# A hybrid decoder step with product-key experts on one core: three more places for tile 0's U rows, 87 dots in the second pass, and the samples' x grouped ahead

## The reference

```
x += W_out [ gMLP-chunk(h) || dilated-window-attention(h) ],  h = RMSNorm(x) W_in
x += PEER(RMSNorm(x));   y = RMSNorm(x)
```

```python
q = (xb @ w_q).reshape(TOK_BLK, PEER_HEADS, 2, DK_HALF)          # 8 heads, 2 halves of 128
s = jnp.einsum('thcd,hcnd->thcn', q, sub_keys)                   # 128 scores per half
s1, i1 = lax.top_k(s[:, :, 0], TOPK); s2, i2 = lax.top_k(s[:, :, 1], TOPK)
cand = (s1[..., :, None] + s2[..., None, :])                     # 16 x 16 sums
top_s, pos = lax.top_k(cand, TOPK)                               # 16 experts per head
eid = jnp.take_along_axis(cid, pos, axis=-1)
g = jax.nn.softmax(top_s, axis=-1)
hid = gelu(jnp.einsum('thkd,td->thk', u_tab[eid], xb))
y = jnp.einsum('thk,thkd->td', g * hid, v_tab[eid])
```

## Time and profile before

| | before |
|---|---|
| median of 3 runs | 1666.52 us (1664.41 to 1666.96) |
| the profiled execution | 1670.37 us |
| its span | 1668.6 us |
| mean granted clock of TensorE | 0.971 |
| busy: PE, DVE, ACT, POOL | 1390.3, 1077.4, 635.6, 654.5 us |
| moved by DMA | 664.81 MB, 398 GB/s over the span |

### The profile page before, as it was taken

How to read it: one execution, slowest core, us unless ns; L and a number is a source line. 1 busy time by engine, 2 the same in 40 slices (tenths; PEclk the granted TensorE clock), 3 DMA queues, 4 the chain that set the end, 5 groups by cost and what they waited for, 6 DMA issues and landing times.

```text
span 1668.6 us, 17631 instructions
## 1 busy us (share of the span) xinstructions
PE 1390.3 (83%) x5164; PEld 616.0 (37%) x5164; DVE 1077.4 (65%) x2770; ACT 635.6 (38%) x1911; POOL 654.5 (39%) x703
## 2 busy tenths in 40 slices
PE   8999995888999988888887877777878777777786
PEld 5585663444334444343322322222223222222211
DVE  1469968877100158677766666666668888888654
ACT  1421113455111045444444544444445444444443
POOL 3035434333467643333343333333333333333331
PEclk9999997899999999999999999999999999999999
DMA  9799989999999999999999999999999999999995
GB/s 340 299 370 383 336 324 395 360 422 382 402 400 400 410 419 419 421 421 421 421 422 421 421 422 421 422 421 421 421 421 420 421 423 417 418 421 414 417 381 246
DMA packets 111567, 664.81 MB, mean 398 GB/s; under 512 B 13008, under 2 KB 14272, under 8 KB 51824
## 3 DMA queue, kind: packets, MB, share of 16 engines
q0 software_dynamic: 97824, 571.76, 84.0%
q1 hardware_dynamic: 13648, 91.93, 13.9%
HBM read 658.04 MB, written 5.60 MB: 398 GB/s over the span
## 4 chain that ended last, share of the span: by engine, by line
DMA 51%; PE 30%; issue 7%; DVE 7%; ACT 5%; POOL 1%; ACTq 0%; DVEq 0%; SPq 0%; POOLq 0%
DMA area_r<-in_uv_tab,eid 41%; PE bank L950 7%; PE bank L667 7%; DMA area_c<-in_uv_tab,eid 5%; PE bank L894 4%; PE bank L939 4%; PE bank L832 3%; ACT area_v L1052 2%; DMA area_r<-in_uv_tab,eidT 1%; DMA area_w<-in_w_out 1%; DMA area_w<-in_uv_tab,eid 1%; PE bank L598 1%; DVE area_r L1759 1%; PE bank L808 1%; DVE area_x L1767 1%
## 5 line engine op out<-in xcount | busy, mean ns | idle before, releaser
L950 PE MATMUL bank<-area_r,area_v 128*128 128x512 f32 (+1 forms) x1032 | 506.1, 620 | 138.5 <-ACT area_v L1052 132.7
L1938 POOL DMA_INDIRECT area_r<-in_uv_tab,eid x383 | 364.4, 951 | 650.6 <-PE bank L950 370.0
L1759 DVE CUSTOM_DVE_ANT_0 area_r<-area_r,bank 128x1024 f32<-128x1024 f32 x275 | 334.5, 1217 | 202.6 <-DMA area_r<-in_uv_tab,eid 202.0
L950 PEld LDWEIGHTS bank<-area_r,area_v 128*128 128x128 f32 (+1 forms) x1032 | 177.9, 187 | 459.2 <-issue 452.8
L1306 ACT ACTIVATE area_v<-hid 128x1 f32<-128x1 f32 x416 | 83.8, 201 | 523.7 <-DVE hid L1759 523.1
L950 PE MATMUL bank<-area_w,area_v 128*128 128x512 f32 (+1 forms) x384 | 190.2, 624 | 54.8 <-ACT area_v L1052 54.5
L1938 POOL DMA_INDIRECT area_w<-in_uv_tab,eid x116 | 110.3, 951 | 179.4 <-PE bank L950 154.0
L667 PE MATMUL bank<-area_w,area_t 128*128 128x384 f32 (+1 forms) x448 | 157.5, 508 | 3.7 <-DMA area_w<-in_w_in 3.1
L1052 ACT ACTIVATE area_v<-ident,area_v 128x128 f32<-128x128 f32 x364 | 146.1, 401 | 33.8 <-PE bank L950 0.4
L1759 DVE CUSTOM_DVE_ANT_0 area_w<-area_w,bank 128x1024 f32<-128x1024 f32 x96 | 116.8, 1217 | 63.7 <-DMA area_w<-in_uv_tab,eid 63.2
L1938 POOL DMA_INDIRECT area_r<-in_uv_tab,eidT x128 | 121.7, 951 | 76.4 <-issue 31.3
(11 more groups left out here) (208 smaller groups left out, 1429.2 us busy)
## 6 DMA issues: line engine op xcount, KB each, us to landing
area_w<-in_w_in SPq DMA_DIRECT2D x12, 1536.0 KB, 10.2
area_w<-in_k_cache SPq DMA_DIRECT2D x8, 1920.0 KB, 11.9
area_w<-in_v_cache SPq DMA_DIRECT2D x8, 1920.0 KB, 10.7
area_w<-in_w_q SPq DMA_DIRECT2D x14, 1024.0 KB, 8.8
area_w<-in_w_out SPq DMA_DIRECT2D x4, 2048.0 KB, 15.2
area_r<-in_uv_tab,eid POOLq DMA_INDIRECT x383, 18.6
area_x<-in_x_p SPq DMA_DIRECT2D x6, 512.0 KB, 17.8
area_w<-in_w_in SPq DMA_DIRECT2D x2, 1024.0 KB, 8.2
```

The lines of the kernel that those rows point to most:

```text
L950: mm = pe.matmul(acc[0:n, c, :], diag[by_pe(i) % DG][:, 0:n], x_ring[s][:, D + c * 512:D + (c + 1) * 512], start=(i == 0), stop=False, ski ...
L1759: vec.tensor_tensor_reduce(out=u, in0=u, in1=x_cur, scale=1.0, scalar=0.0, op0=ALU.mult, op1=ALU.add, accum_out=hid[t % 2][:, j:j + 1]).th ...
L1938: nc.gpsimd.indirect_dma_start(out=place, out_offset=None, in_=table, in_offset=bass.IndirectOffsetOnAxis(ap=where, axis=0)).then_inc(land ...
```

## The change

It has two halves.

Tile 0's rows: three more places, in the part of `area_w` behind the pieces of W_in. Place 9 is where the scores of tile 0's heads 0 to 3 were and is open from row 52 on, place 10 where those of heads 4 to 7 were (from row 108), place 11 the work area of the routing chain (from row 110). The first row of each waits until the scores there are used: `eid_ready` 4 for place 9, 8 for places 10 and 11. The second pass has 87 dots instead of 80. Head 7's chain begins at group 5 of the attention instead of 7. The second load of the query weights, which comes into the area of places 9 and 10, waits in addition for all 128 dots.

The samples: x of the samples is written into a tile of its own (`x_group`, in the place of tile 1's x) by four copies, one in each of the heads 2 to 5 of tile 3, and `set_x` then makes one copy of it. The gathers of pairs have twelve places instead of ten from row 96 on; the two new ones are where the transposed features were (`area_t`).

```diff
--- before.py
+++ after.py
@@ -49,8 +49,8 @@
 TOPK = 16
 SLOTS = HEADS * TOPK
 UR, VR, XR = 6, 12, 6
-U_EXTRA = ((6, 56), (9, 66), (26, 76))
-XR_ALL, X_MORE, X_WIDER = 10, 6, 96
+U_EXTRA = ((6, 56), (9, 66), (26, 76), (52, SLOTS), (108, SLOTS), (110, SLOTS))
+XR_ALL, X_MORE, X_WIDER = 12, 6, 96
 DG = 4
 RING = 3
 
@@ -61,9 +61,9 @@
 FIRST = [sum(STEPS[:t]) for t in range(NT)]
 NSTEP = sum(STEPS)
 
-DOTS_FIRST, DOTS_PROJ = 12, 80
+DOTS_FIRST, DOTS_PROJ = 12, 87
 ROUTE_PROJ = {1: 2, 6: 3, 12: 4, 18: 5}
-ROUTE_ATT = {1: 6, 7: 7}
+ROUTE_ATT = {1: 6, 5: 7}
 ROUTE_STEP = {8: [9, 10]} | {g: [g + 2] for g in range(9, 24)} | {g: [2 * g - 22, 2 * g - 21] for g in range(24, 31)}
 TOPS_ATT, EID_SAMPLE = 15, 5
 EARLY_GROUPS = 8
@@ -121,7 +121,8 @@
         qT = cut(area_r, 0, PAIRS, TOK)
         kT = cut(area_r, PAIRS * TOK, PAIRS, TOK)
         u_ring = [cut(area_r, 2 * PAIRS * TOK + s * D, D) for s in range(UR)]
-        u_extra = [cut(area_w, (s + 1) % RING * PIECE + KD * HALF, D) for s in range(RING)]
+        u_extra = ([cut(area_w, (s + 1) % RING * PIECE + KD * HALF, D) for s in range(RING)]
+                   + [cut(area_w, RING * PIECE + s * D, D) for s in (1, 2, 3)])
 
 
         def u_places():
@@ -140,7 +141,8 @@
         x_ring = ([cut(area_r, s * 2 * D, 2 * D) for s in range(XR // 2)]
                   + [cut(area_r, 2 * PAIRS * TOK + (V_TURN // 2 + s) % (UR // 2) * 2 * D, 2 * D) for s in range(XR // 2)]
                   + [cut(area_c, 0, 2 * D)]
-                  + [cut(area_w, 2 * PIECE + a, 2 * D) for a in (0, WQ, 2 * WQ + D)])
+                  + [cut(area_w, 2 * PIECE + a, 2 * D) for a in (0, WQ, 2 * WQ + D)]
+                  + [cut(area_t, s * 2 * D, 2 * D) for s in range(2)])
         keys = cut(area_r, 2 * PAIRS * TOK + UR * D, 2 * HEADS * NKEYS)
         h_stage = u_ring
         xn_first = u_ring[UR - 1]
@@ -171,6 +173,7 @@
         u_tok = cut(area_v, NT * DB, NT, DA)
         vn = cut(area_v, NT * (DB + DA), NT, DA)
         xn_tile = [xn_first] + [cut(area_v, (t - 1) * D, D) for t in range(1, NT)]
+        x_group = cut(area_v, 0, D)
         y_junk = cut(area_v, NT * D, D)
 
         logc = cut(area_c, 0, 512)
@@ -269,7 +272,7 @@
         q_done, q_copied = [sem(f"q_done{c}") for c in range(2)], [sem(f"q_copied{c}") for c in range(2)]
         s_done, s_ready = sem("s_done"), sem("s_ready")
         tops_exped, tops_less, head_least = sem("tops_exped"), sem("tops_less"), sem("head_least")
-        u_landed = [sem(f"u_landed{s}") for s in range(UR + RING)]
+        u_landed = [sem(f"u_landed{s}") for s in range(UR + len(U_EXTRA))]
         v_landed = [sem(f"v_landed{s}") for s in range(VR)]
         x_landed = [sem(f"x_landed{s}") for s in range(XR_ALL)]
         x_free, hid_ready, bent_ready, col_ready, diag_ready = (sem("x_free"), sem("hid_ready"), sem("bent_ready"),
@@ -570,6 +573,7 @@
             for t in range(2, NT):
                 load_x(t)
             sp.wait_ge(route_link, HEADS * LINKS)
+            sp.wait_ge(u_free, UR + SLOTS)
             for h in range(3):
                 load_wq(wq_ring[h], h, wq_again[h])
             sp.wait_ge(vn_ready, NT)
@@ -1723,8 +1727,7 @@
                 if t < SAMP:
                     ins = vec.tensor_copy(x_cur, xn_tile[t])
                 else:
-                    for g in range(GROUPS):
-                        ins = vec.tensor_copy(x_cur[g * NSAMP:(g + 1) * NSAMP, :], xn_tile[t][0:NSAMP, :])
+                    ins = vec.tensor_copy(x_cur, x_group)
                 then(ins)
 
             def routings(ks):
@@ -1903,6 +1906,9 @@
                     go_on(links)
                     if g == HEADS:
                         finish_head(HEADS + 1)
+                    if t == SAMP - 1 and 2 <= h < 2 + GROUPS:
+                        a = (h - 2) * NSAMP
+                        then(vec.tensor_copy(x_group[a:a + NSAMP, :], xn_tile[SAMP][0:NSAMP, :]))
                     if h == 1:
                         finish_y(t - 1)
                     if g == 30:
@@ -1952,8 +1958,10 @@
                     pool.wait_ge(u_free, UR)
                 elif s < UR + 2:
                     pool.wait_ge(q_done[1], 2 * (s - UR + 2))
+                elif s == UR + 2:
+                    pool.wait_ge(proj_done, units_through(NC))
                 else:
-                    pool.wait_ge(proj_done, units_through(NC))
+                    pool.wait_ge(eid_ready, HEADS // 2 if s == UR + RING else HEADS)
                 gather(u_row(s), single, eid[:, i:i + 1], u_landed[s])
 
             def gather_v(j):
```

## The result

The changed kernel takes 1681.05 us (median of four runs, 1680.37 to 1683.34). The kernel before took 1666.18 us beside it (four runs, 1664.41 to 1666.96). The ratio over the runs of both is 1.0079, with a 95% interval of 1.0065 to 1.0094. The change makes the kernel slower, by 14.9 us between these two medians and by 13.2 us by the ratio; what follows goes by ratios. The forecast was 1660.2 us, faster, with a range that ended at 1668.0.

The account below looks back on a forecast made before the run. The prediction took nearly everything from 412 us on to go by bytes (DMA). Its terms, +2 + 3.7 - 5 - 6.5 - 0.5 = -6.3 us, took the median from 1666.52 to 1660.2 us, range 1652.5 to 1668.

Parts of the forecast that it names:

- The second pass: Projection, 119 to 255 us: seven more dots fit mostly into DVE's waits; last dot about 2 us later, bounds -2 and +6.
- A new wait: Attention, after head 6's numbers: DVE stops for row 96's landing, 3.7 us at best (taken), 11.6 us at worst.
- Rival 3: Slower, chance 0.12: head 6's first row late, wait 11.6 instead of 3.7 us, PE at lower clock; +4.1, 1670.6 us.
- The wait of row 108: Attention: row 108 waits for head 7's numbers, holding POOL for two groups with nine rows out; no stall.
- The deeper ring: Rest of the attention: ring 7 to 9 deep instead of 6, row waits go; -5 us, bounds 0 and 7.7.
- The tail: Attention's end: 4 us off the last V cache load, 2.5 us off the stretch to the last output product; -6.5 us.
- The samples' rows: Samples' boundary, 1590 to 1595 us: one copy replaces four, the slowest engine sets the landings; -0.5 us, bounds -2.6 and 0.
- the mean of the engines: Samples' boundary: if this counts and not the slowest engine, the hole gives 2.6 us; sign: 3 us or more back.
- The four copies in tile 3: Heads 2 to 5: at most 1.23 us each, hidden by DVE's idle time; each delays one gather's issue, sum unchanged.

## Why the prediction was wrong

**The second pass (+2 us, bounds -2 and +6).** The wait of 8.04 us is gone, as forecast. But the last dot of the pass starts at 268.05 instead of 260.82, 7.2 us later, beyond my upper bound. I let three dots come after the old wait and let that wait shrink. In fact DVE catches up with the rows again at the end: rows 84, 85 and 86 wait 4.19, 0.94 and 0.95 us. "Nothing else waits for DVE there" was wrong too: PE's scores of the attention's second group wait for the first masks that stand behind the last dot, 15.06 us instead of 6.42, and the granted clock in 260 to 280 us was 0.50 against 0.62. The runs put 3.2 to 3.5 us on this (0.9991 and 0.9993 against 0.9972, with 0.1% on each of the three). That it is near what I took is luck; its source was another.

**A new wait (+3.7 us, up to 11.6).** This is the step that failed, by the most: 14.3 to 14.7 us in place of 3.7. Place and cause were right: row 96, right after head 6's numbers, GpSimd idle for 18 us ahead of it, and the wait even shorter than forecast (2.28 us; the gather landed in 299.17 - 295.02 = 4.15 us). The price was wrong, because I priced one landing. What the seven dots use up is the stock of rows: before, six rows (88 to 93) are asked for and not yet used when the numbers come; after, one (row 95). The next rows all leave in one burst and land among each other and the V cache load, and "the later gathers follow 1.25 us apart and are wanted less often" took no account of that: rows 99 and 100 wait 3.42 and 3.15 us, the masks behind them come late, and PE stands for 10.46 us. Taking the stop away with all 87 dots in place is worth 14.3 us (head 6 in the pass) or 14.7 us (fewer dots before head 6). Rival 3 had the direction and PE's stop, with 0.12; it put the price into a late landing of row 96, which did not happen.

**The wait of row 108 ("no stall").** Wrong: GpSimd waits 10.81 us, and DVE then waits 2.91, 3.14 and 2.25 us for rows 108, 112 and 113. Of the nine rows that I had out, seven were out when GpSimd stopped and four when the numbers came, and row 108 then took 11.3 us to its dot. Yet by itself this wait costs nothing that can be measured: with head 6 in the pass it has the same 10.81 us, four rows in stock when the numbers come, and 2.76 us of waiting for row 108, and the kernel takes 0.9993, as without that wait (0.9991). With head 7 two groups later it is 21.89 us, no row is left, and 4.5 us are added; at 80 dots and with head 7 in group 7 it is 2.53 us and the kernel is among the fastest.

**The deeper ring (-5 us).** Right in size, but only without the seven dots. With 80 dots one place takes 0.41% off and three take 0.28 to 0.41% (0.9972, 0.9966 and 0.9959 in three kernels that do not differ beyond their intervals), 5 to 7 us. With 87 dots and head 7 in group 7 three places bring nothing (1.0106 with them, 1.0102 without), and the waits for rows that I took to go rise from 11.9 to 25.9 us (19.8 without the last dots of the pass).

**The tail (-6.5 us, 2 to 10).** Wrong. From the last V cache load to the last product it now takes 427.60 - 405.40 = 22.2 us, before 411.85 - 391.95 = 19.9. PE starts on that load 9.6 us after its issue instead of 10.5, so 0.9 us came of my 4. From there to the last product it takes 12.6 us instead of 9.4: the same last products take 1.98 us where they took 1.09, with 0.54 of the clock granted in 420 to 428 us and 1.00 before in 402 to 412. The run with the samples' half alone has 1.98 us there too and no loss of time, so these 3.2 us may be of this execution only. The dots that left the last groups had cost nothing there that can be measured: with 76 dots, four more in the attention, the ratio is that of 80. In those groups they were covered by PE and the caches, which I had not tested by a row.

**The samples' rows (-0.5 us).** Right as far as it can be told: the hole is filled and the time stays (1.000 within 0.001), which leaves room for -0.5 us and for nothing, and none for the 2.6 us by the mean of the engines. In the profiled execution the rows did move by what was forecast: in the run with the samples' half alone six rows take 1606.07 - 1591.19 = 14.9 us where the earlier trace rows had 15.4.

```profile
1591.19 1.22 DVE L1761 CUSTOM_DVE_ANT_0 area_r<-area_r,bank 128x1024 f32<-128x1024 f32 x1 [1.25 <-DMA area_r<-in_uv_tab,eid]
...
1606.07 1.22 DVE L1761 CUSTOM_DVE_ANT_0 area_r<-area_r,bank 128x1024 f32<-128x1024 f32 x1 [1.23 <-DMA area_r<-in_uv_tab,eid]
```

The four copies in tile 3 take 0.67 to 0.94 us each, not 1.23. In the run with the samples' half alone the gather beside one takes 1.31 us where the next one takes 0.94, and the next starts on time all the same (the copy on VectorE, then the two gathers on GpSimd):

```profile
1416.98 0.68 DVE L1910 COPY area_v<-area_v 32x1024 f32<-32x1024 f32 x1
```

```profile
1416.48 1.31 POOL L1943 DMA_INDIRECT area_c<-in_uv_tab,eid  x1 [1.56 <-PE bank L953]
1418.97 0.94 POOL L1943 DMA_INDIRECT area_r<-in_uv_tab,eid  x1 [1.18 <-PE bank L953]
```

The rule of the Trainium skill (SBUF — State Buffer, the box in "SBUF: two separate sides") that such a copy keeps GpSimd from writing descriptors agrees with this. It is seen beside three of the four copies (1.20, 1.31 and 1.30 us), each time with the gather's end 0.13 us behind the copy's. Beside the fourth the gather takes its 0.94 us and the copy 0.94 instead of 0.68. Other gathers between 1330 and 1510 us take up to 1.17 us without such a copy beside them. It costs 0.3 to 0.4 us of a queue that waits over 1 us for the next place anyway, and so changes no time, as the prediction had it.

In sum, the seven dots cost 1.07% with the change's places and head 7 (1.0079 - 0.9972), and 1.02% in the kernel before. Of the 1.07%, some four fifths are the stop at head 6 with too little stock (0.86 to 0.88%, each within about 0.2%); the rest fits the late end of the pass. How the 14 us at head 6 divide between DVE's own waits, PE's stop and its lower clock (0.79 in 300 to 320 us against 0.91) was not taken apart.

## What to carry to other kernels

Before you move work of a consumer forward, count the stock ahead of it: how many items are asked for and not yet used when the next item cannot be asked for. A stop of the requests was nearly free here while the stock lasted, and when it is gone the price is not one landing but a burst of landings in company, with everything that is queued behind the consumer. A place more in a ring and items used sooner pull in opposite directions; try the place alone first.

## What the runs showed that I had not expected

- Similar pauses of the requests (15.25 and 18.18 us), and similar transfers in 280 to 300 us (181 and 148 GB/s), went with times 0.88% apart, by two dots more or less of stock.
- Transfers that ran ahead were given back: with the samples' half alone 417 instead of 379 GB/s in 1580 to 1620 us, then 235 instead of 312, and rows landed some 2.5 us apart all the same. In 1645 to 1650 us it moves 44 GB/s where the kernel before moves 338, and its dots still start 2.47 us apart.
- A gather of 0.52 MB on empty queues landed within 4.15 us of its start, the same form in company in 11.0 us.
- PE's granted clock in 260 to 280 us was 0.50 or 0.51, the level of 1.2 GHz, in all six kernels with 87 dots, where PE had stood 14 to 20 us for the first masks. With 83 dots it was 0.54, behind 10.5 us of standing. With 80 or 76 dots it was 0.62 to 0.76, a mix of both levels, and PE had stood at most 6.4 us.
